# Three root-mean-square norms: two tiles from x times its gain, root row and bias applied when the sums are read, next two tiles in halves

## The reference

```python
def _rmsnorm(x, g):
    y = xf * lax.rsqrt(jnp.mean(xf * xf, axis=-1, keepdims=True) + NORM_EPS)
    return (y * g.astype(jnp.float32)).astype(x.dtype)
...
h = _rmsnorm(x, norm1_g[i]) * (1.0 + sc1) + sh1
...                                   # mixer; layer 1: h @ w_in, split into b_gate, c_gate, u; z = c_gate * u
x = x + g1 * y
h = _rmsnorm(x, norm2_g[i]) * (1.0 + sc2) + sh2
x = x + g2 * ((jax.nn.silu(h @ w_gate) * (h @ w_up)) @ w_down)
```

## Time and profile before

| | us |
|---|---|
| median of three runs | 1737.07 |
| the runs | 1734.59 to 1738.52 |
| span of the profiled execution | 1734.7 |
| TensorE busy in it | 1668.1 (96%) |
| VectorE busy | 1015.6 (59%) |
| ScalarE busy | 703.0 (41%) |
| GpSimd busy | 76.8 (4%) |

### The profile page before, as it was taken

How to read it: one execution, slowest core, us unless ns; L and a number is a source line. 1 busy time by engine, 2 the same in 40 slices (tenths; PEclk the granted TensorE clock), 3 DMA queues, 4 the chain that set the end, 5 groups by cost and what they waited for, 6 DMA issues and landing times.

```text
span 1734.7 us, 23016 instructions
## 1 busy us (share of the span) xinstructions
PE 1668.1 (96%) x7756; PEld 1329.5 (77%) x7756; DVE 1015.6 (59%) x2004; ACT 703.0 (41%) x1329; POOL 76.8 (4%) x61
## 2 busy tenths in 40 slices
PE   6999999999999998888999999999999899999999
PEld 5777777778877775467888888887888788888887
DVE  7788876665467797835655563466454533333334
ACT  5364676653343335753333323234223433332322
POOL 0020000000000073100000000000000000000000
PEclk9999999999999998999999999999999999999999
DMA  6453444444331120002455553352333233333333
GB/s 241 158 158 113 146 153 154 156 149 137 97 97 49 49 86 25 1 25 73 170 193 194 193 195 121 121 182 86 97 97 97 73 98 97 97 97 97 97 97 110
DMA packets 56775, 202.82 MB, mean 117 GB/s; under 512 B 6576, under 2 KB 6704, under 8 KB 56560
## 3 DMA queue, kind: packets, MB, share of 16 engines
q1 hardware_dynamic: 56688, 201.68, 35.5%
HBM read 198.38 MB, written 2.10 MB: 116 GB/s over the span
## 4 chain that ended last, share of the span: by engine, by line
PE 88%; DVE 6%; ACT 2%; issue 2%; DMA 1%; SPq 0%; POOL 0%; DVEq 0%; ACTq 0%; POOLq 0%
PE bank L480 25%; PE bank L482 25%; PE bank L481 25%; PE bank L584 2%; PE bank L639 2%; PE bank L618 1%; PE bank L523 1%; PE bank L524 1%; DVE W_lo L1433 1%; PE bank L538 1%; DVE SB L2042 1%; DVE AW L1447 1%; PE bank L725 1%; PE bank L744 1%; PE bank L526 1%
## 5 line engine op out<-in xcount | busy, mean ns | idle before, releaser
L480 PE MATMUL bank<-H_hi,W_hi 128*128 128x512 f32 x1336 | 534.5, 400 | 3.3 <-DVE W_lo L1433 2.2
L481 PE MATMUL bank<-H_lo,W_hi 128*128 128x512 f32 x1336 | 521.7, 390 | 0.0
L482 PE MATMUL bank<-H_hi,W_lo 128*128 128x512 f32 x1336 | 521.6, 390 | 0.0
L1433 DVE TENSOR_TENSOR W_lo<-RAW,W_hi 128x512 fp32r<-128x512 f32 x538 | 351.4, 692 | 180.6 <-ACT W_hi L919 164.4
L919 ACT ACTIVATE W_hi<-RAW 128x512 fp32r<-128x512 f32 x538 | 317.3, 625 | 271.6 <-PE bank L482 235.3
L480 PEld LDWEIGHTS bank<-H_hi,W_hi 128*128 128x128 f32 x1336 | 251.3, 188 | 73.4 <-issue 19.7
L481 PEld LDWEIGHTS bank<-H_lo,W_hi 128*128 128x128 f32 x1336 | 251.6, 188 | 54.4 <-issue 4.5
L482 PEld LDWEIGHTS bank<-H_hi,W_lo 128*128 128x128 f32 x1336 | 251.4, 188 | 53.2
L482 PE MATMUL bank<-A_hi,W_lo 128*128 128x512 f32 x352 | 137.1, 390 | 0.0
L481 PE MATMUL bank<-A_lo,W_hi 128*128 128x512 f32 x352 | 137.1, 390 | 0.0
L480 PE MATMUL bank<-A_hi,W_hi 128*128 128x512 f32 x352 | 137.1, 389 | 0.0
(11 more groups left out here) (263 smaller groups left out, 2007.8 us busy)
## 6 DMA issues: line engine op xcount, KB each, us to landing
RAW<-weights SPq DMA_DIRECT2D x269, 512.0 KB, 3.7
AW<-ada SPq DMA_DIRECT2D x100, 512.0 KB, 3.7
X<-x_t SPq DMA_DIRECT2D x4, 512.0 KB, 5.5
y_t<-X SPq DMA_DIRECT2D x8, 256.0 KB, 2.0
LW<-lru_w SPq DMA_DIRECT2D x1, 1024.0 KB, 12.6
QX<-QR SPq DMA_DIRECT2D x40, 16.0 KB
CROW<-crow SPq DMA_DIRECT2D x1, 512.0 KB, 10.7
ROPE<-rope SPq DMA_DIRECT2D x1, 512.0 KB, 13.4
```

The costliest lines, as they stand in the source:

```text
L480: pe.matmul(dst, wh, ch(hi, k), start=(k == 0), stop=False)
L481: pe.matmul(dst, wh, ch(lo, k), start=False, stop=False)
L482: mm = pe.matmul(dst, wl, ch(hi, k), start=False, stop=(k == chunks - 1))
L1433: dve.tensor_tensor(W_lo[:, w], RAW[:, c:c + HALF], W_hi[:, w], ALU.subtract).then_inc(lo_done, 1)
```

## The change

For each of the three norms:

- E = x times gain is formed chunk by chunk in the residual tiles: ScalarE gives E_hi behind each square, VectorE E_lo (`gained_rest`) one tile later.
- The first two tiles behind the norm (a and b) are summed from E instead of h (`half`, `behind_norm` on TensorE). The sums of the last square stand behind the third chunk of tile a, the four row transposes behind the first chunk of tile b.
- ScalarE copies the root's row to RROW. VectorE multiplies the banks of a and b with RROW when it reads them (`raw_out`, to TMPA and TMPB). The bias column W shift of each is added by the activation (a) or in the product (b).
- The bias columns: WT, the transposed weights of the two tiles (1 MB per norm, packed ahead of the launch), is loaded to SBUF. TensorE spreads the shift over the partitions with eight transposes (`shift_rows`), behind the fourth residual tile; ScalarE copies them to SHR in two pieces; VectorE takes two products with a sum (`shift_bias`) ahead of the last residual chunk X[7].
- h is formed beside tiles a and b: even chunks as before on VectorE (`normed`), odd ones by a GpSimd product x times RROW, then by ScalarE with gain and shift, then a rounding copy (`normed_hi`). T1 has four buffers.
- The next two tiles (c and d) run in halves: chunks 0 to 3 of c, then of d, then 4 to 7 of c, then of d.
- The modulation of layer 1 moves from behind the last residual tiles to ahead of them.

The diff, cut to its core:

```diff
 # SyncE
+            def shift_weights(idx):
+                if idx == 2:
+                    sp.wait_ge(y_lo_done, 32)
+                else:
+                    sp.wait_ge(bias_done, idx - 2)
+                    sp.wait_ge(h_lo_done, 8 * idx)
+                sp.dma_start(WT[:], wt[idx - 2:idx - 1, :, :].rearrange("a p c -> (a p) c")).then_inc(wt_in, 16)
...
 # TensorE
+            def half(tile, h, hi, lo, need=None, between=None, done=0):
...
+                for k in range(4 * h, 4 * h + 4):
+                    c = sl * HALF + (k % 4) * P
+                    wh, wl = W_hi[:, c:c + P], W_lo[:, c:c + P]
+                    if need is not None:
+                        need(k, 0)
+                    pe.matmul(dst, wh, ch(hi, k), start=(k == 0), stop=False)
+                    mm = pe.matmul(dst, wl, ch(hi, k), start=False, stop=False)
+                    if need is not None:
+                        need(k, 1)
+                    mm = pe.matmul(dst, wh, ch(lo, k), start=False, stop=(k == 7))
...
+            def behind_norm(t0, idx, z):
...
+                for h in range(2):
+                    half(tiles[0], h, E_hi[idx], E_lo, gained, sums if h == 0 else None, 1)
+                for h in range(2):
+                    half(tiles[1], h, E_hi[idx], E_lo, None, rows if h == 0 else None, 1)
+                half(tiles[2], 0, H_hi, H_lo, normed, None, 1)
+                half(tiles[3], 0, H_hi, H_lo)
+                half(tiles[2], 1, H_hi, H_lo, normed, None, 2)
+                half(tiles[3], 1, H_hi, H_lo, None, None, 1)
+
+            def shift_rows(idx, layer, m):
+                pe.wait_ge(mod_done, layer + 1)
+                for k in range(KC):
+                    mm = pe.transpose(ps[5 + k // 4][:, (k % 4) * P:(k % 4 + 1) * P],
+                                      mod(layer, m, k).to_broadcast([P, P]), cs("ident"))
+                mm.then_inc(shift_mm, 1)
...
-            norm_stat(3)
...
-                    linear_pair(t0, pair)
-                    linear(Tile(t0 + 2), hi, lo, own=False)
-                    linear(Tile(t0 + 3), hi, lo)
+                    behind_norm(t0, pair, pair + 1)
...
 # ScalarE
+            def normed_hi(idx, shift, k):
+                slot = ch(T1, k % 4)
+                if k % 2 == 0:
+                    act.wait_ge(t1_done, 8 * 2 + 4 * (idx - 2) + k // 2 + 1)
+                    act.activation(ch(H_hi, k), slot, ACT.Identity, bias=shift(k)).then_inc(h_hi_done, 1)
+                else:
+                    n = 4 * (idx - 2) + k // 2 + 1
+                    act.wait_ge(xr_done, n)
+                    act.activation(slot, slot, ACT.Identity, scale=GAIN[idx](k), bias=shift(k)).then_inc(xg_done, 1)
+                    act.wait_ge(xg_done, n)
+                    act.copy(ch(H_hi, k), slot).then_inc(h_hi_done, 1)
...
+                if q == 0:
+                    root(idx + 1, 1)
+                    split_hi(c, (0,))
+                    act.wait_ge(stat_mm, STAT_ROWS(idx + 1))
+                    act.copy(RROW[:, :], ps[2][:]).then_inc(root_row, 1)
+                    split_hi(c, (1,))
+                    for k in range(3):
+                        normed_hi(idx, SHIFT[idx], k)
+                    split_hi(d, (0,))
+                    normed_hi(idx, SHIFT[idx], 3)
...
+                    act.activation(ch(G1, par), TMPA[:, :], fn, bias=bias(idx, 0)).then_inc(fn_done, 1)
+                    for k in range(4, 8):
+                        normed_hi(idx, SHIFT[idx], k)
+                    split_hi(d, (1,))
...
                     act.wait_ge(x_new, c0 - 8 + k + 1)
                     square(k, c0 + k)
+                    act.activation(ch(E_hi[idx], k), ch(X, k), ACT.Identity, scale=GAIN[idx](k)).then_inc(e_hi_done, 1)
+                    if k == 5:
+                        act.wait_ge(shift_mm, idx - 1)
+                        for h in range(2):
+                            act.copy(SHR[:, h * S:(h + 1) * S], ps[5 + h][:]).then_inc(shift_row, 1)
+                split_hi(Tile(t0 + 9))
...
 # GpSimd
+            for idx in (2, 3, 4):
+                pool.wait_ge(root_row, idx - 1)
+                pool.wait_ge(bias_done, idx - 1)
+                for k in (1, 3, 5, 7):
+                    if k > 4:
+                        pool.wait_ge(h_lo_done, 8 * idx + k - 3)
+                    pool.tensor_tensor(ch(T1, k % 4), ch(X, k), RROW[:, :], ALU.mult).then_inc(xr_done, 1)
 # VectorE
+            def gained_rest(idx, k):
+                dve.wait_ge(e_hi_done, 8 * (idx - 2) + k + 1)
+                dve.scalar_tensor_tensor(out=ch(E_lo, k), in0=ch(X, k), scalar=GAIN[idx](k), in1=ch(E_hi[idx], k),
+                                         op0=ALU.mult, op1=ALU.subtract).then_inc(e_lo_done, 1)
+
+            def shift_bias(idx):
+                dve.wait_ge(shift_row, 2 * (idx - 1))
+                dve.wait_ge(wt_in, 16 * (idx - 1))
+                for which in range(2):
+                    w = WT[:, which * ADA_W:(which + 1) * ADA_W]
+                    link(dve.tensor_tensor_reduce(out=w, in0=w, in1=SHR[:, :], scale=1.0, scalar=0.0, op0=ALU.mult,
+                                                  op1=ALU.add, accum_out=bias(idx, which)))
+                dve.sem_inc(bias_done, 1)
...
+            def behind_norm(t0, idx, product):
+                a, b, c, d = (Tile(t0 + n) for n in range(4))
+                split_lo(b)
+                gained_rest(idx, 7)
+                variance(idx + 1, 1)
+                inverse(idx + 1, 1)
+                split_lo(c, (0,))
+                dve.wait_ge(root_row, idx - 1)
+                normed(idx, 0)
+                normed(idx, 2)
+                raw_out(a, idx, TMPA)
+                dve.sem_inc(tmp_done, 1)
+                normed_rest(idx, 0)
+                split_lo(c, (1,))
+                normed_rest(idx, 1)
+                split_lo(d, (0,))
+                raw_out(b, idx, TMPB)
+                normed_rest(idx, 2)
+                normed_rest(idx, 3)
+                normed(idx, 4)
+                normed(idx, 6)
+                normed_rest(idx, 4)
+                normed_rest(idx, 5)
+                normed_rest(idx, 6)
+                normed_rest(idx, 7)
+                split_lo(d, (1,))
+                product()
...
                     split_lo(tile.next())
+                    if k:
+                        gained_rest(idx, k - 1)
                     if k == 7:
-                        split_lo(Tile(t0 + 9), (0,))
+                        shift_bias(idx)
                     ready(tile)
                     dve.scalar_tensor_tensor(out=ch(X, k), in0=ps[tile.bank][:], scalar=mod(layer, m, k),
                                              in1=ch(X, k), op0=ALU.mult, op1=ALU.add).then_inc(x_new, 1)
...
                     elif layer == 0:
-                        residual(t0, c0, layer, 5, 0)
+                        modulation(1)
+                        residual(t0, c0, layer, 5, 3)
```

More of the change, by code:

```diff
@@ L355, in ch, with bias @@
             return t[:, ds(j * S, n)]
+        def bias(idx, which):
+            return SM[:, 56 + 2 * (idx - 2) + which:57 + 2 * (idx - 2) + which]
         SPN = COL[:, 0:8]
@@ new lines, in behind_norm, with gained, normed, sums @@
+            def behind_norm(t0, idx, z):
+                tiles = [Tile(t0 + q) for q in range(4)]
+                def gained(k, low):
+                    pe.wait_ge((e_hi_done, e_lo_done)[low], 8 * (idx - 2) + k + 1)
+                def normed(k, low):
+                    pe.wait_ge((h_hi_done, h_lo_done)[low], 8 * idx + k + 1)
+                def sums(k):
+                    if k == 2:
+                        square_sums(z, (ch(SQ, 1),), True)
+                def rows(k):
+                    if k == 0:
+                        pe.wait_ge(rinv_done, z + 1)
+                        stat_rows((z % 2) * 24 + 16, 2).then_inc(stat_mm, 1)
+                for h in range(2):
[6 more added lines that the diff above has]
+                half(tiles[3], 1, H_hi, H_lo, None, None, 1)
@@ L868, in _, with segment @@
                        between=early_sums(3) if q == 7 else None)
-            norm_stat(3)
-            def segment(t0, bodies, hi, lo, chunks=KC, first=None, pair=None, sums=None):
+                if q == 3:
+                    shift_rows(2, 0, 3)
+            def segment(t0, bodies, hi, lo, chunks=KC, first=None, pair=None, sums=None, shift=None):
                 def body(i, f, s=None):
@@ L1151, in pair_body @@
                     par = (p0 + q) % 2
[L1152 to L1155, removed]
+                    if idx is not None:
+                        behind_norm(t0, q, fn, pn, par, idx)
+                    else:
                         split_hi(ga.next())
-                    ready(ga)
-                    act.wait_ge(prod_done, pn - 1)
-                    act.activation(ch(G1, par), ps[PAIR_BANK if first else ga.bank][:], fn).then_inc(fn_done, 1)
@@ new lines, in raw_out @@
+            def raw_out(tile, idx, tmp):
```

(8 more changed lines are left out.)

177 lines of the change are left out of this document (116 added, 61 removed).

## The result

The changed kernel takes 1744.34 us (median of 6 runs, 1742.25 to 1747.21) beside 1737.16 for the kernel before on the same chip: ratio 1.0045, 95% interval 1.0035 to 1.0055, 7.2 us slower. The forecast of 1740.8, slower by 3.7, has the sign, and both medians lie in its range (1729 to 1748); its own case (1738 to 1744) is just missed by the first set. The profiled execution has a span of 1741.7, 7.0 above that of before.

What follows compares the result with a forecast made beforehand. TensorE, busy for nearly the whole span, was taken to bound the kernel. 15.1 us won against 5.9 + 9.0 + 3.9 = 18.8 lost made it 3.7 slower, added to the median: 1740.8, range 1729 to 1748.

Steps and rivals of the forecast that it cites:

- its own case: Whole kernel: new waits outweigh the gain, 3.7 us slower at 1740.8, own range 1738 to 1744; chance 0.40.
- What stays or is added on TensorE: TensorE, three norms: last-square sums 2.8 and 0.9, row transposes 2.5, new shift transposes 5.0 us, leaving 15.1 to win.
- Wait 1: Last residual tiles: X[7] comes later, so TensorE waits 0.9, 4.1 and 0.9 us in norms 1 to 3, together 5.9.
- Wait 2: Behind the root's row: VectorE, held up by GpSimd's products, makes TensorE wait for h, 3.0 us per norm, 9.0 together.
- Rival B: Behind the row: GpSimd and VectorE run beside one another, giving 1735 us, no change; chance 0.20.
- Wait 3: The next tile's weights, split late: TensorE waits 2.4, 0.9 and 0.6 us in norms 1, 2 and 3, together 3.9.
- Costed at nothing: WT loads, SP's waits, the moved modulation, ScalarE's second pass on odd chunks and the silu table load: no time added.
- rival D: Norm 2: new waits bring TensorE's lower clock, 1.5 to 2.3 us a time, 4 to 6 together, 1745 to 1747; chance 0.19.
- my own sign: In the norms' stage: a granted clock below 1 would show the forecast's main account wrong; no size given.

Runs made afterwards that it cites:

- the first set: The first six runs of the changed kernel, no further edit, beside the kernel before: median 1744.34 us, ratio 1.0045.
- The experiment on E_hi: Changed kernel with E_hi made behind the next tile's two weight halves on ScalarE, not in front: 1736.82 us, ratio 1.0001 to the kernel before.
- the new order behind the root: Changed kernel with GpSimd's products on VectorE, E_hi and AW sums later, plus row transposes, weight halves, rests and readings reordered: 1729.54 us, ratio 0.9951.

## Why the prediction was right, and where it was not

**What stays or is added on TensorE.** Mis-sized: eight shift transposes take 0.79 us per norm, not 1.68, four rows 0.35, not 0.84. I divided the length of a merged row by its count (0.83/4). That row ends with the whole length of its last transpose (0.42), which the next matmul would overlap, and the lower level began within it (granted 0.50 from 1367.79 on), though I took it for the full clock. Inside a run they follow at 0.109 (here the matmuls around one run of eight are 1.02 apart, instead of 0.23):

```profile
789.08 0.39 PE L518 MATMUL bank<-YA_hi,W_lo 128*128 128x512 f32 x1
789.30 1.03 PE L622 MATMUL bank<-CS,MOD 128*128 128x128 f32 x8
790.10 0.47 PE L516 MATMUL bank<-YA_hi,W_hi 128*128 128x512 f32 x1
```

For three norms the forecast has 7.5 and the trace 3.4, or 3.9 with the 0.09 that the first matmul behind each run loses: 3.6 too dear.

**Wait 1.** Right in place, and in size where it is large: 0.9 / 4.1 / 0.9 forecast; idle 0.17 / 3.85 (0.46 + 1.10 + 2.29) / 0.54 measured, so too dear in norms 1 and 3. X[7] of norm 2 was forecast some 4 us after its tile and came at 3.97; the loop was forecast at 4.5 and takes 4.45. The experiment on E_hi shows which part of the loop is at fault.

**Wait 2.** Right in size: 3.0 forecast per norm; the first half of tile c lasts 3.15 beyond its matmuls in each of the three norms, 2.0 idle and the rest stops. The mechanism, GpSimd and VectorE in turn, is shown for a third of it: without GpSimd 2.1 is left, and with the new order behind the root 0.5, so that half of the wait came from the order of rests, weight halves and readings on VectorE. What GpSimd held up were normed chunks, nine of twelve at 1.80 to 1.91; the rests, for which I had expected 1 to 1.8, took 0.96 at most. Rival B falls.

**Wait 3.** 2.4 / 0.9 / 0.6 forecast; idle 1.92 / 0.47 / 0.32, with a stop of 0.27 each 2.2 / 0.7 / 0.6. Right.

**Costed at nothing.** The modulation cost a wait of 0.46, against the forecast; the run with it moved shows that 0.2 of it counts. The loads of WT landed 5.7 us after issue and nobody waited for them.

**The clock.** This is the step that failed. I gave the lower level no place in my case and put it into rival D with 0.19, in norm 2 and at 1.5 to 2.3 us a time. It came there, at 3.25 with the sums, and in norm 1's tile e at 1.7, which I had not named: 4.9 together, as D had it (4 to 6), and a granted clock below 1 in the stage was my own sign that my case is wrong. I leaned on one row in which TensorE was busy for 0.84 of 2 us at a granted 1.00. The trace of before had a row against it: in norm 1 the lower level came (at 814.83) behind a single wait of 1.51, the eight sums and the first 0.4 us of the next wait.

```profile
813.40:815.90 2.50, 1.08 (x9) 1.00 (x9) 0.96 (x6) 1.46 (x2) 0.00 (x0) 0.79 0.00 0
```

In this stage the lower level followed all seven waits of 2.2 to 2.7 in front of the sums (six profiles), and two of four waits of 1.00. The Trainium skill (TensorE: Matmul & The Clock Gate, Why this matters for your kernels) warns of idle gaps between bursts of matmuls, but of longer ones than these; here the measurement decides.

The sizes offset in part. Transposes and rows were 3.6 too dear; the matmuls at the lower clock (4.4) stood at nothing; and the waits, 18.8 in the forecast, are 13.4 of idle time and 7.4 of stops, 2.0 too cheap. That leaves 2.8, the miss of the trace (6.7 beside 3.8). That the total came nearer than its parts is luck.

## What to carry to other kernels

Removing a gap of the busiest engine is worth its length only if the work laid into it arrives on time: count the pieces of waiting that replace it, and give each its stop (here 0.27 us) beside its idle time. Where an engine loop decides the pace of a stage, first look at the order on the engine that feeds it; here one activation moved by one place was, by the traces, worth as much as the whole change had cost. Don't hand half of an elementwise chain to GpSimd while VectorE reads two SBUF operands beside it: here four chunks took 3.64 us shared and 2.74 on VectorE alone.

## What the runs showed of the hardware

- A stop of TensorE between 128x512 matmuls costs, beside the idle time shown, 0.16 to 0.18 us behind the last matmul and mostly 0.11 (0.08 in norm 2's residual tiles) behind the first, with 0.02 us of idle time as with 1.35. The first is what a matmul's row of 0.39 lasts beyond the 0.23 at which matmuls follow one another. The ends of matmuls in a trace are modelled, so the sum is surer than the share called idle.
- 128x128 transposes follow one another at 0.109 us inside a run of matmuls at the full clock, so that eight cost 0.79.
- The lower clock needs no long gap: it came 2.4 us after a wait of 2.71 had ended and with TensorE at work again, after 1.00 in two of four profiles, and once behind waits of 0.88, 0.20 and 0.24. What tells these from the waits that left the clock up stays open.
- GpSimd's product of 128x512 took 1.32 to 1.78 us beside VectorE, and a VectorE instruction of two SBUF operands that met it 1.80 to 1.91 instead of 0.68. The reading of tile b's bank, with one operand in SBUF, took 0.68 beside such a product, no more than tile a's without one.
